# Output projection token tile by token tile, its norms beside it, and the MLP begun on half of the tokens

## The chip, the cores and the metric

The kernel runs on one core of a Trainium2 chip. The metric is the device time of one launch in microseconds (us). Before the change it is 1835.69 us, the median of three runs (1834.38 to 1842.27).

## What is computed

One layer of a transformer with an attention branch and a state-space branch, for 128 context tokens and 512 latent tokens of width 1024, all in float32. What matters here is the second half of the layer:

```
merged = sigmoid(g_a) * (attn @ w_attn_o) + sigmoid(g_b) * (y @ w_ssd_o)
mix    = merged @ w_out
x      = LN(alpha * x + gate1 * mix, ln1_g, ln1_b)       # LN: mean and variance over the 1024 columns
h      = LN(x) * (1 + scale2) + shift2
ff     = square(relu(h @ w_mlp1 + b_mlp1)) @ w_mlp2 + b_mlp2     # width 4096 between
x      = LN(alpha * x + gate2 * ff, ln2_g, ln2_b)
```

## The kernel before

The five engines run programs of their own, written out by hand in order; they meet only at semaphores. A matrix operand is split into an upper part (rounded to fp32r) and a lower part (the rest), so that a product is three matmuls: upper by upper, upper by lower, lower by upper. Weights come in blocks of 256 columns (1024 KB). SyncE loads a block into one of two slots of `raw`, ScalarE writes the upper part (`split_hi`, L1284, into `whi`), VectorE the lower one (`split_lo`, L1749, into `wlo`), and TensorE multiplies. Slot and parts of block b are b % 2. Tokens lie in five tiles of 128 (t = 0 is the context); activations that are the moving or stationary operand of a product lie turned, features on partitions, in `hh` (upper) and `hl` (lower), 8 slices k of 644 columns (640 tokens and 4 of padding). PSUM has two tensors of four banks, `acc` and `tp`.

The stretch that the change rewrites goes like this.

*Merge.* In four rounds TensorE multiplies y by two column groups (`sub`) of `w_ssd_o`. For each of the eight results VectorE multiplies by the gate (L2231) and adds the attention branch (L2234), ScalarE writes the upper part to `hh[:, k]` (`merged`, L1684), and VectorE the lower one (L2237, signal `merge_ok`). In the last round the splits of `w_out` blocks 0 and 1 stand between: on both ScalarE and VectorE, the split of block 1 comes ahead of the last merge.

*Output projection.* `pe.wait_ge(s["merge_ok"], KT)`, then `n_stream(2, hh, hl)`: the four blocks b of `w_out` in the outer loop, the five token tiles t in the inner one, 24 matmuls of 256 columns a unit, in two PSUM banks by turns. VectorE takes each unit out with the gate (L2258, into `x1[:, t, cols]`). From b = 2 on it also adds alpha * x and gathers statistics, 256 columns at a time.

*Norms.* When the last unit is out, VectorE goes over all tiles: means and deviations (`gathered`, `deviations`; the root is ScalarE's, L1291), the weighed norm (`weighed`, L1787 and L1788) and new statistics (`statistics`, L1767, L1769) tile by tile, deviations again, and the second norm (`normed`, L1791) into `xq`.

*Turn and modulation.* For each k TensorE turns five 128 by 128 pieces (`turn_x`, L847) into PSUM, ScalarE applies scale and shift (L1327, once for the 128 context tokens and once for the 512 latent ones) and writes the upper part (L1331), VectorE the lower one (`split_h`, L1825, signal `h2_ok`).

*MLP.* TensorE waits for all eight `h2_ok`. In four rounds it makes eight units of 48 matmuls of 322 columns (`t_unit`; each of the two halves of the tokens has its own bank), VectorE and ScalarE take them out with bias, relu and square (L2294, L2296, L1719, L2299, signal `ff_ok`), and then TensorE makes 4 x 5 units of the second product.

Of the kernel before, what the change touches and what calls it, by code (L numbers as in the profile page):

```python
# [6 lines left out]
F32 = mybir.dt.float32  # L7
# [6 lines left out]
P = 128  # L14
# [91 lines left out]
def build(nc, a, outs):  # L106
# [16 lines left out]
    with ExitStack() as ctx:  # L123
# [36 lines left out]
        class Carve:  # L160
# [134 lines left out]
        hf2 = cst[:, P:P + 2 * TP].rearrange("p (a b) -> p a b", a=2)  # L295
        lnr = c7(2, D)
        lnr2 = raw[:, 0].rearrange("p (a k) n -> p a (k n)", a=2)
        xq = c7(NT, D)

        acc = ctx.enter_context(nc.psum_tensor("acc", [P, 4, 512], F32))  # L300
        tp = ctx.enter_context(nc.psum_tensor("tp", [P, 4, 512], F32))

# [5 lines left out]
            conv_out0 conv_out1 dt_in dt_split dt_hi dt_mm dt_copied dt_turned dt_abs dt_soft dt_sums dt_summed  # L308
            dt_exp dt_ok dt_ln acst_ok acs_out kcr_in kct_out rot_ok
# [8 lines left out]
            merge_hi merge_ok gate_turned gate_copied gate_out rows2_in x1_ok h2_hi h2_ok relu_ok square_ok  # L318
# [18 lines left out]
        U_H2 = U_OUT + 4 * NT  # L337
        U_MLP = U_H2 + KT

# [20 lines left out]
        GATED = {8 + 2 * q: q for q in range(4)}  # L360

# [11 lines left out]
        def _(sp):  # L373
# [64 lines left out]
            sp.wait_ge(s["dt_hi"], 1)  # L438
# [211 lines left out]
            sp.wait_ge(s["h2_ok"], KT)  # L650
# [148 lines left out]
        def _(pe):  # L799
# [120 lines left out]
            pe.wait_ge(s["dt_split"], 1)  # L920
# [7 lines left out]
            last.then_inc(s["dt_mm"], 1)  # L928
# [28 lines left out]
            pe.wait_ge(s["dt_copied"], 1)  # L957
            for t in range(NT):
                last = pe.transpose(tp[:, 2, t * 2 * NH:(t + 1) * 2 * NH], dtt[:, tok(t):tok(t) + P], ident[0:2 * NH, 0:2 * NH])
            last.then_inc(s["dt_turned"], 1)  # L960
            qkv_block(1)
            pe.wait_ge(s["dt_sums"], 1)
# [8 lines left out]
            last.then_inc(s["dt_summed"], 1)  # L971
            qkv_block(2)
            pe.wait_ge(s["dt_ok"], 1)
# [289 lines left out]
            with rounds(pe, 4, (lo, 8), (ready, KT + 4 * NT), (free, KT + 4 * NT), (ff, KT)):  # L1263
                for n in range(KT):
                    if n % 2 == 0:
                        pe.wait_ge(lo["sem"], due(lo))
                    t_unit(n // 2 % 2, n % 2, n % 2, hh, hl)
                for n in range(KT):
                    pe.wait_ge(ff["sem"], due(ff))
                for b in range(4):  # L1270
                    pe.wait_ge(lo["sem"], due(lo))
                    n_block(b % 2, fh, fl)

        @block.scalar
        def _(act):
# [131 lines left out]
            act.activation(wdh[:], wdt, ACT.Copy).then_inc(s["dt_hi"], 1)  # L1407
            act.activation(alg, alg, ACT.Exp).then_inc(steps["sem"], step(steps))
            act.wait_ge(s["dt_mm"], 1)
            act.activation(dtt.rearrange("p (a b) -> p a b", a=2), tp[0:2 * NH, 0:2, 0:HALF], ACT.Copy).then_inc(s["dt_copied"], 1)  # L1410
# [23 lines left out]
            def decays_in(n):  # L1434
# [6 lines left out]
            act.wait_ge(s["dt_abs"], 1)  # L1441
            act.activation(dtu[:, 1], dtu[:, 0], ACT.Exp, scale=-1.0).then_inc(steps["sem"], step(steps))
            act.wait_ge(steps["sem"], value(steps))
            act.activation(dtu[:, 1], dtu[:, 1], ACT.Ln, bias=1.0).then_inc(s["dt_soft"], 1)
            block_out(1, q5[:, 1])
            act.wait_ge(s["dt_sums"], 1)
            act.activation(dtu[:, 1], dtu[:, 0], ACT.Ln).then_inc(s["dt_ln"], 1)
            act.wait_ge(s["dt_summed"], 1)
            act.activation(dec[:].rearrange("p t j h -> p j t h"),
                           tp[:, 1:4, 0:NT * 2 * NH].rearrange("p j (t h) -> p j t h", t=NT), ACT.Exp).then_inc(s["dt_exp"], 1)  # L1450
# [7 lines left out]
            act.wait_ge(s["dt_ok"], 1)  # L1458
# [241 lines left out]
            merge_round(3, split_hi)  # L1700

            with rounds(act, 2, (ready, 2 * NT), (hi, 2), (raws[0], 1), (raws[1], 1)):
                for b in range(2):
                    step(ready, NT)
                    act.wait_ge(ready["sem"], value(ready))
                    split_hi(b)
            roots(mv[:, :, 2])
            roots(mv[:, :, 2])
            jump(free, U_H2)
            act.wait_ge(s["pad_ok"], 2)  # L1710
            modulated(hf2, "h2_hi", "h2_ok", 4, 3)
# [24 lines left out]
        def _(dve):  # L1736
# [136 lines left out]
            dve.wait_ge(s["dt_hi"], 1)  # L1873
            dve.tensor_tensor(wdl[:], wdt, wdh[:].bitcast(F32), ALU.subtract).then_inc(s["dt_split"], 1)
# [39 lines left out]
            dve.wait_ge(s["dt_turned"], 1)  # L1914
            do(dve.tensor_tensor(dtu[:, 2], tp[:, 2, 0:NT * 2 * NH].rearrange("p (t h) -> p t h", t=NT), mid(dtb), ALU.add))
            do(dve.tensor_scalar(dtu[:, 0], dtu[:, 2], -1.0, None, ALU.mult))
            dve.tensor_tensor(dtu[:, 0], dtu[:, 0], dtu[:, 2], ALU.max).then_inc(s["dt_abs"], 1)
            do(dve.tensor_scalar(dtu[:, 2], dtu[:, 2], 0.0, None, ALU.max))
            squared(0)
            dve.wait_ge(s["dt_soft"], 1)  # L1920
# [3 lines left out]
            dve.tensor_scalar(dta[:], dta[:], -1.0, None, ALU.mult).then_inc(s["dt_sums"], 1)  # L1924
# [6 lines left out]
            dve.wait_ge(s["dt_exp"], 1)  # L1931
            dve.wait_ge(s["dt_ln"], 1)
# [3 lines left out]
            dve.tensor_tensor(sdt, dts[:], sdt, ALU.mult).then_inc(s["dt_ok"], 1)  # L1936
            dve.wait_ge(s["dt_ok"], 1)
# [286 lines left out]
            def merge_round(i, split):  # L2224
                split(0)
                for b in range(2):
                    dve.wait_ge(ready["sem"], due(ready))
                    if b == 1:
                        split(1)
# [12 lines left out]
            merge_round(3, split_lo)  # L2242

            dve.wait_ge(s["g1_in"], 32)

            def with_x(t, b):

                cols = slice(b * BW, (b + 1) * BW)
                do(dve.scalar_tensor_tensor(x1[:, t, cols], xo[:, t, cols], ALPHA, x1[:, t, cols], ALU.mult, ALU.add))
                dve.bn_stats(st6[:, t, b], x1[:, t, cols])  # L2250

            for b in range(4):
                cols = slice(b * BW, (b + 1) * BW)
                if b == 2:
                    dve.wait_ge(s["rows2_in"], 16 * 5)
                for t in range(NT):
                    dve.wait_ge(ready["sem"], due(ready))
                    dve.tensor_tensor(x1[:, t, cols], acc[:, 2 * ((NT * b + t) % 2), 0:BW],  # L2258
                                      g1r[:, min(t, 1), cols], ALU.mult).then_inc(free["sem"], step(free))
                    if b >= 2:  # L2260
                        dve.wait_ge(free["sem"], value(free))
                        with_x(t, b - 2)
                        with_x(t, b)
                split_lo(b % 2)
            for buf in (hf2[:, :, CTX:CTX + 2], hf2[:, :, NCONV:TP]):
                last = dve.memset(buf, 0.0)
            last.then_inc(s["pad_ok"], 1)
            for t in range(NT):
                gathered(t)
            deviations()  # L2270
            for t in range(NT):
                do(weighed(t, x1[:, t], lnr))
                statistics(t, x1[:, t])
            deviations()
            for t in range(NT):
                normed(t, xq[:, t], x1[:, t]).then_inc(s["x1_ok"], 1)
# [84 lines left out]
```

## Time and profile before

| | us |
|---|---|
| median of three runs | 1835.69 |
| the profiled execution, device time | 1839.19 |
| its span in the profile | 1837.5 |
| TensorE matmul busy in the span | 1632.3 (89%) |
| VectorE busy | 1031.7 (56%) |
| ScalarE busy | 663.7 (36%) |
| share of TensorE in the chain that ended last | 74% |

In the rows, PE is TensorE's matmul, PEld its weight load, DVE is VectorE, ACT ScalarE, SP SyncE. Times count from the start of the span. A releaser ("<-") is the instruction whose signal ended a wait.

### The profile page before, as it was taken

To read this page: it belongs to the slowest core of one execution; us is meant where nothing else is said; L and a number is where in the kernel's file an instruction comes from. 1 tells how busy PE (TensorE), PEld (TensorE's weight loads), DVE (VectorE), ACT (ScalarE), POOL (GpSimd) and SP (SyncE) were. 2 spreads that over 40 slices of the span, in tenths; PEclk is the share of its full clock that TensorE was granted. 3 is DMA by queue.
4 is the path that set the end of the run, shared out by engine and by line. 5 is a ranking of instruction groups with operands and counts; after the bars stand their busy time and mean duration, and the time that the engine had idled before them with its cause. 6 is when DMAs were issued, how large, how long until landed. Compare 5 with 4: busy or idle time off the path is not lost.

```text
span 1837.5 us, 27440 instructions
## 1 busy us (share of the span) xinstructions
PE 1632.3 (89%) x11141; PEld 1538.5 (84%) x11141; DVE 1031.7 (56%) x1419; ACT 663.7 (36%) x1115; POOL 99.3 (5%) x155
## 2 busy tenths in 40 slices
PE   4799999989998998989799899989299999999995
PEld 2699988889998988888655699989199999999995
DVE  5466666556845578887555353335843343342467
ACT  4544443334365246667355432311321121111210
POOL 1000012110011100000000001000000000000000
PEclk9799999899999999999899999999599999999998
DMA  9344345532486676676600255342011222223221
GB/s 309 99 134 136 124 142 187 174 116 75 138 264 206 221 241 213 200 240 189 236 23 23 71 184 179 112 174 70 23 44 56 84 68 68 68 68 91 69 68 57
DMA packets 159721, 241.14 MB, mean 131 GB/s; under 512 B 8048, under 2 KB 126560, under 8 KB 156576
## 3 DMA queue, kind: packets, MB, share of 16 engines
q1 hardware_dynamic: 136464, 171.45, 28.8%
q0 software_dynamic: 12304, 47.72, 7.0%
q10 hardware_dynamic: 10880, 20.97, 4.2%
q8 instruction: 49, 0.80, 0.2%
q14 instruction: 24, 0.20, 0.0%
HBM read 195.06 MB, written 45.06 MB: 131 GB/s over the span
## 4 chain that ended last, share of the span: by engine, by line
PE 74%; DVE 14%; ACT 7%; issue 2%; DMA 1%; SPq 0%; ACTq 0%; DVEq 0%
PE acc L806 66%; PE tp L806 6%; DVE arena L1849 2%; ACT arena L1510 1%; DVE wlo L1749 1%; PE tp L1188 1%; DVE arena L2002 1%; ACT whi L1284 1%; DMA arena<-in_w_mod 1%; DVE arena L1788 1%; DVE arena L1787 1%; PE tp L889 1%; DVE wlo L1800 1%; DVE arena L2004 1%; DMA y_nat<-arena 1%
## 5 line engine op out<-in xcount | busy, mean ns | idle before, releaser
L806 PE MATMUL acc<-hh,whi 128*128 128x322 f32 x1408 | 363.4, 325 | 16.6 <-DVE wlo L1749 7.2
L806 PE MATMUL acc<-hl,whi 128*128 128x322 f32 x1408 | 357.4, 321 | 0.0
L806 PE MATMUL acc<-hh,wlo 128*128 128x322 f32 x1408 | 354.9, 319 | 0.0
L806 PEld LDWEIGHTS acc<-hh,whi 128*128 128x128 f32 x1408 | 254.1, 198 | 18.7 <-issue 12.2
L806 PEld LDWEIGHTS acc<-hl,whi 128*128 128x128 f32 x1408 | 255.2, 198 | 0.0
L806 PEld LDWEIGHTS acc<-hh,wlo 128*128 128x128 f32 x1408 | 254.1, 197 | 0.0
L1284 ACT ACTIVATE whi<-raw 128x2048 fp32r<-128x2048 f32 x78 | 148.7, 1908 | 266.2 <-PE acc L806 266.2
L1749 DVE TENSOR_TENSOR wlo<-raw,whi 128x2048 fp32r<-128x2048 f32 x78 | 178.5, 2290 | 101.5 <-ACT whi L1284 101.2
L806 PE MATMUL acc<-whi,hh 128*128 128x256 f32 x720 | 206.9, 287 | 8.0 <-DVE hl L2237 8.0
L806 PE MATMUL acc<-whi,hl 128*128 128x256 f32 x720 | 203.6, 283 | 0.0
L806 PE MATMUL acc<-wlo,hh 128*128 128x256 f32 x720 | 203.6, 283 | 0.0
L806 PE MATMUL acc<-whi,fh 128*128 128x256 f32 x640 | 183.2, 286 | 15.2 <-DVE fl L2299 15.2
L806 PE MATMUL acc<-wlo,fh 128*128 128x256 f32 x640 | 183.3, 286 | 0.0
L806 PE MATMUL acc<-whi,fl 128*128 128x256 f32 x640 | 182.8, 286 | 0.0
L806 PEld LDWEIGHTS acc<-whi,hh 128*128 128x128 f32 x720 | 137.4, 191 | 8.8 <-issue 8.4
L806 PEld LDWEIGHTS acc<-whi,fh 128*128 128x128 f32 x640 | 124.5, 195 | 16.3 <-issue 16.3
L806 PEld LDWEIGHTS acc<-wlo,hh 128*128 128x128 f32 x720 | 137.0, 190 | 0.3
L806 PEld LDWEIGHTS acc<-whi,hl 128*128 128x128 f32 x720 | 137.0, 190 | 0.0
L806 PE MATMUL tp<-arena 128*128 128x64 f32 (+3 forms) x508 | 115.6, 373 | 15.0 <-DVE arena L2004 10.0
L806 PEld LDWEIGHTS acc<-wlo,fh 128*128 128x128 f32 x640 | 124.3, 194 | 0.0
L806 PEld LDWEIGHTS acc<-whi,fl 128*128 128x128 f32 x640 | 124.2, 194 | 0.0
L1849 DVE SCALAR_TENSOR_TENSOR arena<-arena,colp 128x642 f32<-128x642 f32 x128 | 113.7, 888 | 18.7 <-DVE arena L1847 1.2
(255 smaller groups left out, 2327.0 us busy)
## 6 DMA issues: line engine op xcount, KB each, us to landing
raw<-in_w_in SPq DMA_DIRECT2D x38, 1024.0 KB, 7.0
raw<-in_w_mlp SPq DMA_DIRECT2D x32, 1024.0 KB, 5.4
arena<-in_w_mod SPq DMA_DIRECT2D x24, 1024.0 KB, 6.3
arena<-decay_sums_t ACTq DMA_DIRECT2D x40, 512.0 KB, 5.5
arena<-xs_nat SPq DMA_DIRECT2D x8, 1024.0 KB, 8.0
raw<-in_w_ssd_o SPq DMA_DIRECT2D x8, 1024.0 KB, 6.0
y_nat<-arena POOLq DMA_DIRECT2D x6, 1024.0 KB, 7.2
arena<-y_nat SPq DMA_DIRECT2D x6, 1024.0 KB, 6.4
```

The source lines that it names most:

```text
L806: return pe.matmul(out, l, r, start=first, stop=last)
L889: last = pe.transpose(dst, cvs[:, n % 2, tok(t):tok(t) + P], ident)
L1188: last = pe.transpose(tp[:, j // 4, (j % 4) * P:(j % 4 + 1) * P], pr[:, u, j * P:(j + 1) * P], ident)
L1284: act.activation(whi[:, slot], raw[:, slot], ACT.Copy).then_inc(hi["sem"], step(hi))
L1510: last = act.activation(ee[:, b, d, r], abc[:, b, d, r], ACT.Relu, bias=dta[:, c, h:h + 1], scale=-1.0)
L1749: dve.tensor_tensor(wlo[:, slot], raw[:, slot], whi[:, slot].bitcast(F32), ALU.subtract).then_inc(lo["sem"], step(lo))
L1787: do(dve.scalar_tensor_tensor(x, x, mv[:, t, 0:1], rows[:, 0], ALU.subtract, ALU.mult))
L1788: return dve.scalar_tensor_tensor(x, x, mv[:, t, 2:3], rows[:, 1], ALU.mult, ALU.add)
L1800: dve.tensor_tensor(dst, src, upper.bitcast(F32), ALU.subtract).then_inc(mlo["sem"], step(mlo))
L1849: ins = dve.scalar_tensor_tensor(o, x[:, t:t + NCONV], w(t), o, ALU.mult, ALU.add)
L2002: last = dve.tensor_tensor(ee[:, b, d], ee[:, b, d], cbm[:, d, g].unsqueeze(1).broadcast_to([P, R, P]), ALU.mult)
L2004: dve.tensor_tensor(ee[:, b, 0], ee[:, b, 0], ee[:, b, 1], ALU.add).then_inc(m_ok["sem"], step(m_ok))
```

## The change

- **Last merges first.** In the last merge round ScalarE and VectorE do both merges before they split block 1 of `w_out`. TensorE no longer waits for all eight merges: units 0 and 1 of the output projection run over k = 0 to 6, each k behind its own `merge_ok`, and take k = 7 at their end.
- **Output projection by tiles.** The order of the twenty units becomes `OUT`: tiles 0, 1 and 2 mixed as far as the blocks arrive, then tile 3 and tile 4 with their four blocks each. All four blocks must now be kept: blocks 2 and 3 get parts of their own, `w2h` and `w2l`, where the operand of the merge product lay. The units go round four banks of `acc`.
- **Norms per tile.** VectorE takes units out (`gated_out`) and does, one tile behind the other, `summed` (add alpha * x over 1024 columns, statistics), `normed_once` (weighed norm, statistics) and `normed_twice` (the two numbers of the second norm). The second norm itself moves to ScalarE, which writes `xq`. The roots are per tile too, ten instead of two.
- **Turn and modulation per tile.** TensorE turns tile 0 behind unit 10, tile 1 behind unit 14, tile 2 behind unit 17, into `tp`; ScalarE modulates in eight instructions of 128 columns and writes the upper part in one of 1024 (`modulate`), VectorE the lower part in one (`lower`).
- **MLP from half the tokens.** Columns 0 to 321 hold the tokens of tiles 0, 1 and part of 2. TensorE waits for three tiles (`h2_ok` 3), makes the first halves of MLP units 0 to 3, turns tile 3 behind the first of them and tile 4 behind the last, and then makes the second halves. Units 2 and 3 use the banks of `tp` (`pair_of`), as every second pair of MLP units does now. For tile 4 VectorE does half of the modulation (`lower_last`).
- **Loads.** x, the weights of the norm and the bias row are asked for behind block 3 of `w_out`, in another order; their landing signals are split in two.
- Twelve semaphores of the dt stage become three, with the same order of waits.

```diff
@@ SyncE @@
+            sp.wait_ge(s["acc_ready"], U_OUT)
+            sp.dma_start(xo[:, 0], a["x_prompt"][0]).then_inc(s["xo_in"], 16)
+            sp.dma_start(lnr[:, 0], a["ln1_g"][0].partition_broadcast(P)).then_inc(s["xo_in"], 16)
+            sp.dma_start(lnr[:, 1], a["ln1_b"][0].partition_broadcast(P)).then_inc(s["xo_in"], 16)
+            sp.dma_start(xo[:, 1:NT], a["x_sample"][0].rearrange("(t p) d -> p t d", p=P)).then_inc(s["rows2_in"], 16)
             sp.wait_ge(s["merge_ok"], KT)
-            sp.wait_ge(s["acc_ready"], U_OUT)
-            sp.dma_start(xo[:, 0], a["x_prompt"][0]).then_inc(s["rows2_in"], 16)
-            sp.dma_start(xo[:, 1:NT], a["x_sample"][0].rearrange("(t p) d -> p t d", p=P)).then_inc(s["rows2_in"], 16)
-            sp.dma_start(lnr[:, 0], a["ln1_g"][0].partition_broadcast(P)).then_inc(s["rows2_in"], 16)
-            sp.dma_start(lnr[:, 1], a["ln1_b"][0].partition_broadcast(P)).then_inc(s["rows2_in"], 16)
             sp.dma_start(row, a["b_mlp2"][0].partition_broadcast(P)).then_inc(s["rows2_in"], 16)
@@ TensorE @@
+        OUT = [(0, 0), (1, 0), (2, 0), (0, 1), (1, 1), (0, 2), (0, 3), (1, 2), (1, 3), (2, 1), (2, 2), (2, 3)]
+        OUT += [(t, b) for t in range(3, NT) for b in range(4)]
+        TURN = {10: 0, 14: 1, 17: 2}
-            pe.wait_ge(s["merge_ok"], KT)
-            n_stream(2, hh, hl)
-            turn_x(xq, "x1_ok", NT)
-            pe.wait_ge(s["h2_ok"], KT)
+            for i in range(2):
+                out_begun(i, seen)
+                out_products(i, range(KT - 1))
+            for i in range(2):
+                out_products(i, [KT - 1]).then_inc(ready["sem"], step(ready))
+            for i in range(2, 4 * NT):
+                out_begun(i, seen)
+                out_products(i, range(KT)).then_inc(ready["sem"], step(ready))
+                if i in TURN:
+                    turn_tile2(TURN[i])
+            pe.wait_ge(s["h2_ok"], 3)
+            for n in range(4):
+                if n % 2 == 0:
+                    pe.wait_ge(lo["sem"], due(lo))
+                ...
+                half_unit(n, 0)
+                if n == 0:
+                    turn_tile2(NT - 2)
+            pe.wait_ge(s["acc_free"], U_OUT + 4 * NT)
+            turn_tile2(NT - 1)
+            pe.wait_ge(s["h2_ok"], NT)
+            for n in range(4):
+                half_unit(n, 1).then_inc(ready["sem"], step(ready))
+            for n in range(4, KT):
+                mlp_unit(n)
+            second_products()
+            with rounds(pe, 3, (lo, 8), (ready, KT + 4 * NT), (free, KT + 4 * NT), (ff, KT)):
+                for n in range(KT):
+                    mlp_unit(n)
+                second_products()
@@ ScalarE @@
-            merge_round(3, split_hi)
+            act.wait_ge(half["sem"], due(half))
+            split_hi(0)
+            gate_in(0)
+            gate_in(1)
+            merged(KT - 2)
+            merged(KT - 1)
+            step(ready, 2)
+            act.wait_ge(ready["sem"], value(ready))
+            split_hi(1)
+            for b in range(2):
+                act.wait_ge(raws[b]["sem"], due(raws[b]))
+                act.activation(w2h[:, b], raw[:, b], ACT.Copy).then_inc(hi["sem"], step(hi))
+            for t in range(NT):
+                roots(mv[:, t, 2:3])
+                if t:
+                    modulate(t - 1)
+                if t == NT - 2:
+                    act.wait_ge(ready["sem"], U_OUT + 17)
+                    split_hi(0)
+                roots(mv[:, t, 2:3])
+                if t == NT - 2:
+                    act.wait_ge(ready["sem"], U_OUT + 18)
+                    split_hi(1)
+                act.wait_ge(s["n2_ok"], t + 1)
+                act.activation(xq[:, t], x1[:, t], ACT.Identity, bias=mv[:, t, 3:4], scale=mv[:, t, 2:3]).then_inc(s["x1_ok"], 1)
+            modulate(NT - 1)
@@ VectorE @@
+            split_lo(1)
+            split_out_lo(0)
+            gated_out(3)
+            split_out_lo(1)
+            gated_out(4)
+            summed(0)
+            gated_out(1)
+            normed_once(0)
+            gated_out(1)
+            normed_twice(0)
+            summed(1)
+            gated_out(1)
+            normed_once(1)
+            gated_out(2)
+            for t in range(2, NT - 1):
+                lower(t - 2)
+                normed_twice(t - 1)
+                summed(t)
+                gated_out(2)
+                normed_once(t)
+                gated_out(2 if t == 2 else 1)
+            lower(2)
+            split_lo(0)
+            gated_out(1)
+            normed_twice(NT - 2)
+            summed(NT - 1)
+            split_lo(1)
+            normed_once(NT - 1)
+            normed_twice(NT - 1)
+            lower(NT - 2)
+            lower_last()
```

## Rows read from the trace of the kernel before

**Rows 1.** TensorE's waits, 1200 to 1400 us: waiter, releaser, total us, times, longest.
```profile
PE acc L847 <- DVE arena L1791: 32.3, 1, 32.3
PE acc L806 <- DVE hl L2237: 8.0, 1, 8.0
PE acc L806 <- DVE hl L1825: 4.2, 1, 4.2
PE acc L806 <- DVE fl L2299: 3.8, 1, 3.8
PE acc L847 <- ACT cst L1327: 2.5, 6, 0.5
```

**Rows 2.** Stretches: length, busy us (instructions) of PE, PEld, DVE, ACT, POOL; PEclk; DMA.
```profile
1220.60:1228.50 7.90, 0.02 (x1) 0.03 (x1) 4.68 (x4) 2.60 (x2) 0.00 (x0) 0.77 0.29 90
1228.50:1233.20 4.70, 4.70 (x28) 4.70 (x29) 0.08 (x1) 0.00 (x0) 0.00 (x0) 0.67 1.02 362
1233.20:1286.80 53.60, 53.56 (x455) 53.35 (x453) 28.74 (x59) 5.76 (x4) 0.00 (x0) 1.00 0.32 112
1286.80:1319.00 32.20, 0.00 (x0) 0.00 (x0) 30.52 (x50) 3.61 (x4) 0.00 (x0) 0.54 0.11 33
1319.00:1336.10 17.10, 10.36 (x40) 7.56 (x40) 10.05 (x14) 14.17 (x24) 0.00 (x0) 0.50 0.01 1
1336.10:1345.80 9.70, 9.66 (x50) 9.67 (x51) 0.00 (x0) 0.00 (x0) 0.00 (x0) 0.75 0.00 0
1345.80:1395.70 49.90, 49.90 (x336) 49.71 (x334) 24.72 (x24) 10.62 (x10) 0.00 (x0) 1.00 0.20 64
...
1399.60:1405.80 6.20, 6.19 (x29) 6.20 (x30) 2.71 (x2) 0.65 (x1) 0.00 (x0) 0.51 0.31 103
```

**Rows 3.** Chain that ended last, around the last merge: start, length, engine, line.
```profile
1220.56 1.92 ACT whi L1284
1222.60 2.29 DVE wlo L1749
...
1227.29 0.84 DVE hl L2237
...
1228.48 58.29 PE acc L806 x480
```

**Rows 4.** TensorE's turns in the chain, inside the attention projection (y).
```profile
1052.91 1.75 PE tp L1234 x16
```

**Rows 5.** DMA issues, 1224 to 1231 us: size of one, median us to landing.
```profile
raw<-in_w_out SPq DMA_DIRECT2D x1, 1024.0 KB, 5.1
...
arena<-in_b_mlp SPq DMA_DIRECT2D x1, 512.0 KB, 11.9
```

**Rows 6.** VectorE and ScalarE by form, 1289 to 1345 us: busy us, mean ns.
```profile
L1767 DVE BATCH_NORM_STATS2 st<-arena 128x6 f32<-128x512 f32 x10 | 6.4, 685 | 0.2
L1788 DVE SCALAR_TENSOR_TENSOR arena<-arena,mv 128x1024 f32<-128x1024 f32 x5 | 6.4, 1285 | 0.2
L1787 DVE SCALAR_TENSOR_TENSOR arena<-arena,mv 128x1024 f32<-128x1024 f32 x5 | 6.4, 1285 | 0.2
L1327 ACT ACTIVATE cst<-acc,modc 128x512 f32<-128x512 f32 x8 | 6.2, 769 | 0.0
...
L1327 ACT ACTIVATE cst<-acc,modc 128x128 f32<-128x128 f32 x8 | 3.5, 444 | 5.6 <-PE acc L847 5.6
...
L1769 DVE BATCH_NORM_AGGREGATE mv<-st 128x2 f32<-128x12 f32 x5 | 1.0, 209 | 0.2
...
L1777 DVE TENSOR_SCALAR mv<-mv 128x5 f32<-128x5 f32 x2 | 0.3, 172 | 0.1
```

**Rows 7.** VectorE's instructions by form over the whole span: busy us, mean ns.
```profile
L1749 DVE TENSOR_TENSOR wlo<-raw,whi 128x2048 fp32r<-128x2048 f32 x78 | 178.5, 2290 | 101.5 <-ACT whi L1284 101.2
...
L2258 DVE TENSOR_TENSOR arena<-acc,arena 128x256 f32<-128x256 f32 x20 | 8.4, 422 | 25.8 <-PE acc L806 25.7
...
L1910 DVE TENSOR_TENSOR arena<-arena,cst 128x1024 f32<-128x1024 f32 x5 | 6.1, 1226 | 0.2
```

**Rows 8.** ScalarE in order of time, 1319 to 1324 us: start, length of the pair.
```profile
1322.32 1.11 ACT L1327 ACTIVATE cst<-acc,modc 128x128 f32<-128x128 f32 x2
```

More of the change, by code:

```diff
@@ L1256, in _ @@
                     t_pass(1, sub, sub, yh, yl, KT, False, True).then_inc(ready["sem"], step(ready))
-            pe.wait_ge(s["merge_ok"], KT)
-            n_stream(2, hh, hl)
-            turn_x(xq, "x1_ok", NT)
-            pe.wait_ge(s["h2_ok"], KT)
-            ff = count(s["ff_ok"])
[L1263 to L1267, printed above, removed]
+            blocks = [(whi[:, 0], wlo[:, 0]), (whi[:, 1], wlo[:, 1]), (w2h[:, 0], w2l[:, 0]), (w2h[:, 1], w2l[:, 1])]
@@ new lines, in turn_tile2, with out_products @@
+            def turn_tile2(t):
+                pe.wait_ge(s["x1_ok"], t + 1)
+                if t >= 2:
+                    pe.wait_ge(s["h2_hi"], t - 1)
+                for k in range(KT):
+                    last = pe.transpose(turned_at(t, k), xq[:, t, k * P:(k + 1) * P], ident)
+                last.then_inc(s["h2_turned"], 1)
+            def out_products(i, ks):
+                t, b = OUT[i]
+                for k in ks:
+                    if i == 0:
+                        pe.wait_ge(s["merge_ok"], k + 1)
+                    for m, w in ((hh, 0), (hh, 1), (hl, 0)):
+                        last = mul(acc[:, i % 4, 0:BW], m[:, k, tok(t):tok(t) + P], blocks[b][w][:, k],
+                                   k == 0 and w == 0 and m is hh, k == KT - 1 and m is hl)
+                return last
@@ new lines, in mlp_unit @@
+            def mlp_unit(n):
+                if n % 2 == 0:
+                    pe.wait_ge(lo["sem"], due(lo))
+                step(free)
+                pe.wait_ge(free["sem"], value(free, 2))
+                for k in range(KT):
+                    for w, m in ((whi, hh), (whi, hl), (wlo, hh)):
+                        for half in range(2):
+                            last = mul(pair_of(n)[:, half, 0:HALF], w[:, n // 2 % 2, k, n % 2 * P:(n % 2 + 1) * P],
+                                       m[:, k, half * HALF:(half + 1) * HALF], k == 0 and w is whi and m is hh, k == KT - 1 and w is wlo)
+                last.then_inc(ready["sem"], step(ready))
@@ L2265, in _, with split_out_lo @@
[L2265 to L2271, printed above, removed]
+            def split_out_lo(b):
+                dve.wait_ge(hi["sem"], due(hi))
+                dve.tensor_tensor(w2l[:, b], raw[:, b], w2h[:, b].bitcast(F32), ALU.subtract).then_inc(lo["sem"], step(lo))
+            units = count(s["acc_ready"])
@@ new lines, in gated_out, with variance @@
+            def gated_out(n):
+                for i in range(units["k"], units["k"] + n):
+                    t, b = OUT[i]
+                    cols = slice(b * BW, (b + 1) * BW)
+                    dve.wait_ge(ready["sem"], due(ready))
+                    dve.tensor_tensor(x1[:, t, cols], acc[:, i % 4, 0:BW], g1r[:, min(t, 1), cols], ALU.mult).then_inc(free["sem"], step(free))
+                step(units, n)
+            def variance(t):
+                dve.tensor_scalar(mv[:, t, 2:3], mv[:, t, 1:2], EPS, None, ALU.add).then_inc(var["sem"], step(var))
@@ new lines, in summed, with normed_once @@
+            def summed(t):
+                dve.wait_ge(free["sem"], value(free))
+                if t == 0:
+                    dve.wait_ge(s["xo_in"], 48)
+                if t == 1:
+                    dve.wait_ge(s["rows2_in"], 32)
+                do(dve.scalar_tensor_tensor(x1[:, t], xo[:, t], ALPHA, x1[:, t], ALU.mult, ALU.add))
+                statistics(t, x1[:, t])
+                variance(t)
+            def normed_once(t):
+                dve.wait_ge(dev["sem"], due(dev))
+                do(dve.reciprocal(mv[:, t, 2:3], mv[:, t, 2:3]))
@@ L2272, in _, with normed_twice @@
                 do(weighed(t, x1[:, t], lnr))
                 statistics(t, x1[:, t])
[L2274 to L2276 removed]
+                variance(t)
+            def normed_twice(t):
+                dve.wait_ge(dev["sem"], due(dev))
+                do(dve.reciprocal(mv[:, t, 2:3], mv[:, t, 2:3]))
+                dve.scalar_tensor_tensor(mv[:, t, 3:4], mv[:, t, 0:1], -1.0, mv[:, t, 2:3], ALU.mult, ALU.mult).then_inc(s["n2_ok"], 1)
```

167 lines of the change are left out of this document (97 added, 70 removed).

## The prediction

> **What bounds the kernel now.** I read the waits of TensorE first, because it is 89% busy and every microsecond in which it stands still is likely to be on the path. In the stretch of the change they are few and long [rows 1]: 8.0 us for the lower part of the last merge (L2237), 32.3 us for the second norm (L1791), 2.5 us in six pieces inside the turn, and 4.2 us for the last lower part before the MLP (L1825). The 3.8 us for L2299 recur in each MLP round and are not touched.
>
> The stretches [rows 2] then say what lies around the waits. From 1233.2 to 1286.8 the output projection runs at the full clock (granted 1.00), 19 units in 53.6 us, 2.82 us each; VectorE is busy 28.7 of these 53.6 us and ScalarE 5.8, so both have room. From 1286.8 to 1319.0 TensorE does nothing and VectorE is busy 30.5 of 32.2 us. From 1319.0 to 1336.1 there are 40 turns at half clock, held to ScalarE's pace (14.2 of 17.1 us busy). The first MLP unit then takes 9.7 us (to 1345.8), and the seven that follow 49.9 us, 7.13 each. So from the end of the merge products, 1220.5, to the end of MLP unit 3 (1345.8 + 3 x 7.13 = 1367.2) there pass **146.7 us**. That is what I compare with; what comes behind unit 3 does not change.
>
> The chain [rows 3] shows why the last merge is late: it goes through ScalarE's split of block 1 (1.92 us from 1220.56) and VectorE's (2.29 us from 1222.60), and only then through the merge, which ends at 1228.1.
>
> **The change, part by part.** TensorE's own work after it, from 1220.5: 20 units x 2.82 = 56.4 us; five tiles turned, 8 turns each, with 16 turns in 1.75 us at full clock [rows 4], 5 x 0.88 = 4.4 us; eight half units = four units, 28.5 us. Together 89.3 us. To this come the waits, which I go through in order.
>
> *Last merge.* Units 0 and 1 over k = 0 to 6 last 2 x 7/8 x 2.82 = 4.9 us, to 1225.4. The merge now begins at 1220.5. In [rows 3] it takes from the end of the split (about 1224.8) to 1228.1, 3.3 us, so it is done at 1223.9. No wait; the cover is 1.5 us. The 8.0 us go, and with them the slow clock behind them.
>
> *Blocks 1 to 3.* ScalarE splits block 1 behind the last merge, 1223.0 to 1224.9, VectorE to 1227.2; unit 3 needs it at 1228.9. The upper part of block 2 follows on ScalarE, its lower part on VectorE is done at 1229.5, needed by unit 5 at 1234.5. Block 3 can be loaded only when VectorE has split block 1 (1227.2, where it was 1224.9). A block landed 5.1 us after its issue [rows 5]: 1232.4; 1.92 and 2.29 us for its parts [rows 3] give 1236.7. Unit 6 wants it at 1237.4. No wait, 0.7 us of cover. x and the norm rows are issued behind it; the last of that burst landed 11.9 us after its issue [rows 5]; with one block more ahead of it I say 15 us, so all is there by about 1244, and tile 1 wants it at about 1250. The blocks of the MLP queue behind and are wanted at 1279.
>
> *VectorE becomes the limit.* Unit 6 completes tile 0 at 1220.5 + 7 x 2.82 = 1240.2. From there on VectorE has no pause until TensorE may begin the MLP. Per tile: `summed` is one operation over 1024 columns and two half statistics, 1.29 + 2 x 0.66 + 0.21, with gaps and the 0.17 us of a tiny operation behind it 3.1 us; `normed_once` is a tiny one, two operations of 1.29 us and the same statistics, 4.6 us; `normed_twice` two tiny ones, 0.4 us [rows 6]. `lower` over 1024 columns is 1.25 us, taking out a unit 0.45 us, a split 2.29 us, each with its gap [rows 7]. Up to the lower part of MLP block 0 stand in its program 4 x 3.1 + 4 x 4.6 + 3 x 0.4 + 3 x 1.25 + 13 x 0.45 + 2.3 = 43.9 us: done at **1284.1**. TensorE by itself would be there at 1220.5 + 20 x 2.82 + 3 x 0.88 = 1279.5. **It waits 4.6 us.**
>
> ScalarE must not be late between. Eight modulations of 128 columns: one lasts 0.444 us [rows 6], and since a pair of 128 and 512 columns takes 1.11 us [rows 8] where the sum of both is 1.21, a series of eight is 0.34 to 0.44 us a piece, 2.8 to 3.6 us. The upper part over 1024 columns is about half of the 1.92 us for 2048 and some, 1.1; `xq`, by the step from 128 to 512 columns, 1.2. With the roots that is 5.5 to 6.3 us a tile; VectorE's share is 11. In the order of the waits the closest case is the second root of tile 2, which stands behind the modulation of tile 1: that ends at about 1269 and VectorE asks for the root at 1269. VectorE then still has units to take out and a lower part to write (2.1 us) before it needs the answer. So nothing.
>
> Here a rule of the Trainium skill speaks against the change: "VectorE: DVE Perf Modes", in its section on the TRN2 errata, says that ScalarE and VectorE pay a fixed cost for every instruction and wants tiles of 512 elements or more. The two forms of L1327 agree: from 512 to 128 columns the time falls only from 0.769 to 0.444 us. By the rule ScalarE's modulation rises from 9.7 us to about 36 x 0.44 = 16 us, but behind VectorE's longer program that changes no term.
>
> *First halves and last tile.* From 1284.1: half unit 0 3.57 us, tile 3 turned 0.9, half units 1 to 3 10.7 us. The clock will be low after a wait of 4.6 us: after the 3.8 us wait before 1399.6, 29 matmuls in 6.2 us ran at granted 0.51, which at full clock (0.118 us each) are 3.4 us, a loss of 2.8; after the 8.0 us wait the first unit lost 1.9 (4.7 us where 2.82 would do); the first MLP unit lost 9.7 - 7.13 = 2.6 us [rows 2]. I take 2.0 here. TensorE is ready to turn tile 4 at 1301.3. VectorE meanwhile: one unit out, 0.4, 3.1, a split 2.3, 4.6, 0.4 = 11.3 us, to 1295.4, then `xq` 1.2: 1296.6. So the last tile's norms are hidden, with 4.7 us of cover. What isn't: the turn, then on VectorE four operations of 128 columns (0.3 each), a copy and two subtractions of 512 (0.5 to 0.7 each): **3.1 us**. ScalarE's half (4 x 0.34 + 0.6) is shorter. I add 1.5 us for the clock again, less than before since the wait is shorter, and 0.5 us at MLP unit 4, which waits for VectorE to take out unit 2 behind a weight split.
>
> The sum: 89.3 + 4.6 + 2.0 + 3.1 + 1.5 + 0.5 = **101.0 us** instead of 146.7: 45.7 us less. The profiled execution would go from 1839.2 (1.7 us outside its span) to 1793.5. It lies 3.5 us above the median of the runs; the median would go to 1835.7 - 45.7 = **1790**.
>
> Bounds of what no row has. Clock losses: none to 2.8 each, -3.5 to +2.1 us. The many small steps of VectorE 7% cheaper or 10% dearer: -2.4 to +4.7. ScalarE's 128-column instructions: cheaper ones gain nothing; as dear as the 512-column form (6.1 us a tile), they push VectorE back by 4.9. The MLP keeps four waits of 3.8 us, whose clock losses (2.3 to 2.8) can fall otherwise by 2 us in all. Units 4 and later in other banks of `tp`: nothing, since the wait is still for the unit two back. The longer straight program of TensorE: nothing, since the attention and y stretch is written out too and runs its turns without gaps [rows 4]. The joined semaphores: nothing, the same order.
>
> **Rivals.** (a) *Block 3 lands late.* Its cover is 0.7 us, and the burst goes out in its back. For it: in [rows 5] the burst's last load took 11.9 us. Against: block 3 is asked for first. If it lands 3 to 7 us late, unit 6 waits 2 to 6 us, everything behind shifts, and the clock loses 2 more: 1794 to 1798.
>
> (b) *The two engines lock step.* ScalarE and VectorE hand roots, `n2_ok` and lower parts back and forth, each in program order; if each tile costs VectorE 2 to 4 us of waiting, four times, the limit moves from 1284 to 1292 or 1300, and with it everything behind: 1798 to 1806. Against it stand ScalarE's 5.5 to 6.3 us beside VectorE's 11.
>
> (c) *The output projection at half clock.* The new units wait on free banks and blocks, four banks round. If TensorE stood a little before every unit, its clock might stay at the 1.2 GHz level. The 29 slow matmuls in 6.2 us give 0.213 us against 0.118: over 480 matmuls 45.6 us, over 192 of the half units about 23 more, less the 4.6 us that TensorE then need not wait: 1790 + 64 = 1854, slower than before. It decides from about 480 slow matmuls on, the whole of the projection. Against: with the two-bank order the clock is 1.00 for 53.6 us without a break [rows 2], and my ledger has no wait in it. "TensorE: Matmul & The Clock Gate" in the Trainium skill, section on psum-queue depth-cycling, describes such a kernel, in which going round the PSUM banks leaves small pauses and the clock swings.
>
> (d) *The change does less than it says:* the first halves start only when the last tile is ready, as if there were no halves. Then the 14.3 us of first halves no longer lie beside the last tile's norms; less their present cover of 4.7 us that is 9.6 more: 1800. For it: the wait for tile 2's lower part and the block's split may drift towards the end of VectorE's program. Against: in that program they stand 11.3 us ahead of its last tile.
>
> **Chances.** The forecast, every wait as in the ledger within a few us: 0.70, its own range 1784 to 1797. (a) 0.10, (b) 0.10, (d) 0.03, (c) 0.02, and 0.05 for a larger gain, below 1784, if VectorE is quicker and the clock hardly falls. The range 1782 to 1802 leaves out (c), half of (b) and part of the last. A change of 0.5%, 9 us, is about what a measurement of this kernel can tell from none; only (c) and something like it would end there: faster 0.96, same 0.02, slower 0.02.
>
> **What would show it.** TensorE's waits between 1220 and 1320: no entry for the merge; one of about 4.6 us before the first half unit, released by L1749's split; one of about 3.1 before the second halves, released by the last lower part; none inside the twenty units. VectorE nearly without pause from 1240 to 1284. The granted clock 1.00 from 1216 to about 1279. MLP unit 3 ended at about 1321.5. I am wrong if the units of the projection show waits for blocks or for `x1_ok`, or if VectorE waits for ScalarE by more than 1 or 2 us in all from 1240 to 1284.

## The result

The changed kernel takes **1791.82 us** (median of 4 runs, 1787.32 to 1797.25) against 1835.75 us: a ratio of 0.9759, 95% interval 0.9741 to 0.9778, so 43.9 us less. The forecast was 1790. The profiled execution took 1791.86 us with a span of 1790.2.

TensorE's waits after it, from the last merge product to MLP unit 4 and the first `ff_ok`: waiter, releaser, total us, times, longest.

```profile
PE acc L821 <- DVE fl L2478: 4.0, 1, 4.0
PE acc L821 <- DVE hl L2428: 3.4, 1, 3.4
PE acc L821 <- issue: 2.6, 1, 2.6
PE acc L821 <- DVE cst L2473: 0.6, 1, 0.6
```

Of the four entries of [rows 1] that the change aims at, 47.0 us together, nothing is left under those names. There are two new waits, 2.6 us before the first half unit and 3.4 us before the second halves (L2428, the last lower part), and 0.6 us at MLP unit 4. The 4.0 us for L2478 is the old 3.8 us of L2299.

The stretches after it, with the columns of [rows 2]:

```profile
1216.10:1228.00 11.90, 11.90 (x103) 11.90 (x102) 7.97 (x8) 4.35 (x3) 0.00 (x0) 1.00 0.35 112
1228.00:1247.10 19.10, 19.10 (x164) 19.10 (x163) 14.12 (x24) 4.85 (x5) 0.00 (x0) 1.00 0.88 317
1247.10:1272.00 24.90, 24.90 (x215) 24.90 (x214) 23.14 (x45) 13.61 (x32) 0.00 (x0) 1.00 0.01 2
1272.00:1277.90 5.90, 3.34 (x29) 3.13 (x27) 5.58 (x9) 5.36 (x6) 0.00 (x0) 1.00 0.00 0
1277.90:1283.30 5.40, 5.37 (x26) 5.39 (x27) 5.26 (x9) 1.45 (x2) 0.00 (x0) 0.68 0.62 197
...
1294.80:1299.10 4.30, 0.92 (x9) 0.68 (x7) 3.23 (x8) 2.13 (x5) 0.00 (x0) 0.97 0.00 0
1299.10:1303.00 3.90, 3.90 (x17) 3.90 (x18) 3.33 (x5) 0.00 (x0) 0.00 (x0) 0.60 0.00 0
...
1315.70:1344.50 28.80, 28.80 (x192) 28.59 (x192) 16.15 (x16) 7.33 (x7) 0.00 (x0) 1.00 0.35 110
```

From 1216.1, the end of the merge products, TensorE runs to 1272 without a pause at granted 1.00; VectorE is busy 23.1 of the 24.9 us from 1247.1 to 1272.0, where it had been busy 28.7 of 53.6 [rows 2]. Behind the two waits the clock is at 0.68 and 0.60.

The forecast went wait by wait, and so does the comparison. From the last merge product to the start of MLP unit 4:

| term | forecast us | measured us |
|---|---|---|
| wait for the last merge | 0 | 0 |
| 20 units and 3 turned tiles | 59.0 | 59.2 (1216.1 to 1275.3) |
| 8 half units and 2 turned tiles at full clock | 30.3 | 30.3 (what the other rows leave) |
| wait before the first half unit | 4.6 | 2.6 |
| clock lost in it | 2.0 | 1.8 (5.4 where 3.57 would do) |
| wait before the second halves | 3.1 | 3.4 |
| clock lost behind it | 1.5 | 1.7 (16.0 from 1299.1 to 1315.1 where 14.3 would do) |
| wait at unit 4 | 0.5 | 0.6 |
| whole stretch | 101.0 | 99.6 (1216.1 to 1315.7) |

The stretch is 47.1 us shorter, the span 47.3. The part ahead was also 4.4 us shorter in this execution (the merge products ended at 1216.1, in [rows 2] at about 1220.5), and the part behind 4.2 us longer. Nothing shows the first to be an effect of the change: in the nine executions of the changed kernel and its variants profiled below this moment lies anywhere from 1212.5 to 1221.0, and in those of the kernel before and its two variants at 1220.5, 1216.0 and 1218.0. The second is an effect, and the forecast did not have it; the last experiments are about it.

VectorE in order of time, at the places that decide (start us, length, idle before and its releaser):

```profile
1216.13 0.83 DVE L2354 SCALAR_TENSOR_TENSOR arena<-arena,acc 128x644 f32<-128x644 f32 x1 [3.85 <-PE acc L821]
...
1218.63 0.83 DVE L2360 SCALAR_TENSOR_TENSOR hl<-arena,hh 128x644 fp32r<-128x644 f32 x1 [0.81 <-ACT hh L1778]
...
1230.38 2.29 DVE L2372 TENSOR_TENSOR out_lo<-raw,out_hi 128x2048 fp32r<-128x2048 f32 x1 [4.38 <-ACT out_hi L1819]
...
1235.89 0.42 DVE L2381 TENSOR_TENSOR arena<-acc,arena 128x256 f32<-128x256 f32 x1 [2.23 <-PE acc L821]
...
1252.37 0.15 DVE L2385 TENSOR_SCALAR mv<-mv 128x1 f32<-128x1 f32 x1
1252.44 0.74 DVE L2381 TENSOR_TENSOR arena<-acc,arena 128x256 f32<-128x256 f32 x2
1253.10 1.22 DVE L2413 TENSOR_TENSOR hl<-arena,hh 128x1024 fp32r<-128x1024 f32 x1
1254.23 0.16 DVE L2407 RECIPROCAL mv<-mv 128x1 f32<-128x1 f32 x1
1254.43 0.16 DVE L2408 SCALAR_TENSOR_TENSOR mv<-mv 128x1 f32<-128x1 f32 x1
1254.50 1.22 DVE L2394 SCALAR_TENSOR_TENSOR arena<-arena 128x1024 f32<-128x1024 f32 x1
...
1264.35 1.23 DVE L2413 TENSOR_TENSOR hl<-arena,hh 128x1024 fp32r<-128x1024 f32 x1 [0.76 <-ACT hh L1815]
...
1274.11 1.21 DVE L2413 TENSOR_TENSOR hl<-arena,hh 128x1024 fp32r<-128x1024 f32 x1
1275.54 2.29 DVE L1872 TENSOR_TENSOR wlo<-raw,whi 128x2048 fp32r<-128x2048 f32 x1 [0.21 <-ACT whi L1378]
...
1295.77 1.37 DVE L2421 TENSOR_SCALAR arena<-acc,modc 128x128 f32<-128x128 f32 x4 [5.96 <-PE acc L1280]
...
1298.36 0.69 DVE L2428 TENSOR_TENSOR hl<-arena,hh 128x512 fp32r<-128x512 f32 x1
```

The last merge starts at 1216.13 and its lower part ends at 1219.5, 3.3 us as forecast, when TensorE still has 1.5 us of k = 0 to 6 to do. Block 3 is split to 1232.7; its first unit was due at 1233.0, so about 0.3 us of cover were left where I had 0.7. At 1274.11 comes tile 2's lower part, then the split of MLP block 0, to 1277.83. TensorE's rows there:

```profile
1275.06 0.28 PE L821 MATMUL acc<-out_hi,hl 128*128 128x256 f32 x1
1277.93 0.39 PE L821 MATMUL acc<-hh,whi 128*128 128x322 f32 x1 [2.60 <-issue]
```

The view says "issue", as if nothing had held it, but the start at 1277.93 lies 0.1 us behind the end of the split, on whose signal the code waits. A releaser is inferred; the end times show it better here.

ScalarE (eight modulations and an upper part of tile 0, and the last `xq`):

```profile
1248.10 2.90 ACT L1811 ACTIVATE arena<-tp,modc 128x128 f32<-128x128 f32 x8 [0.17 <-PE tp L1280]
1251.03 1.06 ACT L1815 ACTIVATE hh<-arena 128x1024 fp32r<-128x1024 f32 x1
...
1288.70 1.25 ACT L1832 ACTIVATE arena<-arena,mv 128x1024 f32<-128x1024 f32 x1 [0.42 <-DVE mv L2408]
```

Eight modulations take 2.90 us, 0.36 each, inside the 0.34 to 0.44 of the forecast. The last `xq` is done at 1289.95, and TensorE turned that tile only at 1294.69:

```profile
1294.69 1.04 PE L1280 MATMUL acc<-cst,arena 128*128 128x128 f32 x8
```

That is 4.7 us of cover, as forecast.

### The profile page after: what moved, and what is told of

It is laid out like the page before. It is cut to its first block, busy times and chain, and to the rows that moved or that the text cites. A ratio compares the mean times of both kernels' runs of the same rounds, so it can differ in the third digit from the quotient of the medians.

```text
span 1790.2 us, 27388 instructions
## 1 busy us (share of the span) xinstructions
PE 1619.5 (90%) x11141; PEld 1528.4 (85%) x11141; DVE 1026.0 (57%) x1409; ACT 674.6 (38%) x1145; POOL 99.2 (6%) x155
## 4 chain that ended last, share of the span: by engine, by line
PE 75%; DVE 13%; ACT 7%; issue 3%; DMA 1%; SPq 0%; ACTq 0%; DVEq 0%
PE acc L821 60%; PE tp L821 12%; DVE arena L1972 2%; ACT arena L1604 2%; PE tp L1203 1%; DVE wlo L1872 1%; DVE arena L2125 1%; ACT whi L1378 1%; DMA arena<-in_w_mod 1%; PE tp L904 1%; DVE wlo L1923 1%; DVE arena L2127 1%; DMA y_nat<-arena 1%; ACT arena L1390 0%; ACT whi L1741 0%
## 5 line engine op out<-in xcount | busy, mean ns | idle before, releaser
L821 PE MATMUL acc<-hh,whi 128*128 128x322 f32 x1152 | 305.6, 327 | 22.7 <-DVE wlo L1872 7.2
L821 PE MATMUL acc<-hl,whi 128*128 128x322 f32 x1152 | 299.4, 321 | 0.0
L821 PE MATMUL acc<-hh,wlo 128*128 128x322 f32 x1152 | 297.5, 320 | 0.0
L821 PEld LDWEIGHTS acc<-hh,whi 128*128 128x128 f32 x1152 | 209.9, 199 | 25.3 <-issue 15.2
L821 PEld LDWEIGHTS acc<-hl,whi 128*128 128x128 f32 x1152 | 210.8, 198 | 0.0
L821 PEld LDWEIGHTS acc<-hh,wlo 128*128 128x128 f32 x1152 | 210.1, 198 | 0.0
L821 PE MATMUL acc<-whi,hh 128*128 128x256 f32 x640 | 183.8, 287 | 0.0
L821 PE MATMUL acc<-whi,hl 128*128 128x256 f32 x640 | 180.5, 282 | 0.0
L821 PE MATMUL acc<-wlo,hh 128*128 128x256 f32 x640 | 180.4, 282 | 0.0
L1390 ACT ACTIVATE arena<-acc 128x644 f32<-128x644 f32 (+2 forms) x94 | 47.8, 510 | 194.9 <-PE acc L821 194.8
```

The costliest lines, as they stand in the source:

```text
L821: return pe.matmul(out, l, r, start=first, stop=last)
L1390: act.activation(dst, src, func).then_inc(free["sem"], step(free))
```

## Experiments

All are compared with the kernel before on the same chip; medians of five or more runs. Ratios are to that kernel, and the changed kernel's own is 0.9759 (0.9741 to 0.9778). Because the front part drifts by some microseconds, I read the waits first and the medians second. "Stretch" below is from the last merge product until VectorE takes out MLP unit 4; it is 108.5 us in the changed kernel (109.6 in its second profile), 153.9 before. It ends later than the 99.6 us of the table above, which end where TensorE starts on unit 4.

No experiment takes back the tile order with the norms beside it, the largest part of the change. What it is worth rests on the traces: one wait of 32.3 us before, one of 2.6 us after.

### The order of the last merges alone

```diff
 (kernel before, ScalarE)
-            merge_round(3, split_hi)
+            act.wait_ge(half["sem"], due(half))
+            split_hi(0)
+            gate_in(0)
+            gate_in(1)
+            merged(KT - 2)
+            merged(KT - 1)
+            step(ready, 2)
+            act.wait_ge(ready["sem"], value(ready))
+            split_hi(1)
 (VectorE: the split of block 1 behind the last merge, too)
```

> The kernel before, with the order of the last merge round alone changed: both engines do the last merge before they split block 1. Theory (the last merge is late because it stands behind the two splits, 1.92 and 2.29 us in the chain): TensorE's wait at the start of the output projection falls from 8.0 to about 3.6 us, and the time by 4 to 5 us, to about 1831 us. Rival (the merge itself, or the gate's load, is what is late): the wait stays near 8 us and the time does not move.

1830.44 us, ratio 0.9966 (0.9950 to 0.9982).

```profile
PE acc L806 <- DVE hl L2245: 3.7, 1, 3.7
```

The wait went from 8.0 to 3.7 us, as the theory has it. The medians give 3 to 9 us by the interval, the wait 4.3, and the stretch is about 4 us shorter (150.1).

### The old order inside the changed kernel, and no early products

```diff
 (e5_old_merge_order, ScalarE; VectorE likewise)
             merged(KT - 2)
-            merged(KT - 1)
             step(ready, 2)
             act.wait_ge(ready["sem"], value(ready))
             split_hi(1)
+            merged(KT - 1)
 (e6_all_merges, TensorE)
-                        pe.wait_ge(s["merge_ok"], k + 1)
+                        pe.wait_ge(s["merge_ok"], KT)
```

> The changed kernel with the old order of the last merge round (block 1 split before the last merge), but TensorE still beginning units 0 and 1 with k = 0 to 6. Theory: these products cover 4.9 us, the merge is done about 7.6 us after the last merge product, so a wait of about 2.7 us appears in unit 0, with up to 2 us of clock behind it: 1794 to 1797 us. Rival (VectorE's chain alone sets when the MLP begins, so anything in front of it is hidden): 1792, no change.

> The changed kernel, but TensorE waits for all eight merges before unit 0 (the new order of the merges stays). Theory: the 3.4 us of the merge become a wait, and the clock may fall behind it for another 1 to 2 us: 1795 to 1797 us. Rival (the order alone does it, beginning with k = 0 to 6 is worth nothing, because VectorE's chain takes up the slack): 1792.

Old order: 1796.59 us, ratio 0.9784 (0.9759 to 0.9808). No early products: 1802.29 us, ratio 0.9807 (0.9780 to 0.9834). TensorE's wait for the last merge in the first and in the second:

```profile
PE acc L821 <- DVE hl L2360: 2.7, 1, 2.7
```

```profile
PE acc L821 <- DVE hl L2360: 3.6, 1, 3.6
```

2.7 and 3.6 us, where 2.7 and 3.4 were expected, and the other waits (2.6, 3.4, 0.6) keep their lengths behind it. So VectorE's chain does not swallow what is lost in front: its work hangs on unit 6, and unit 6 moves. With the old order the stretch is 111.6 us, 2 to 3 longer; the median lies in the expected range, but its interval overlaps that of the changed kernel. The stretch without early products is 113.6 us, 4 to 5 longer. Its median missed the expected 1795 to 1797 by 5 us; in its profiled execution, which is the median one, 5 us of the difference lie ahead of the stretch (merge products ended at 1221.0, in the changed kernel at 1216.1).

### No first halves

```diff
 (the loop over four first halves, with both turns, goes; in its place:)
+            turn_tile2(NT - 2)
+            pe.wait_ge(s["acc_free"], U_OUT + 4 * NT)
+            turn_tile2(NT - 1)
+            pe.wait_ge(s["h2_ok"], NT)
             for n in range(4):
+                if n % 2 == 0:
+                    pe.wait_ge(lo["sem"], due(lo))
+                half_unit(n, 0)
                 half_unit(n, 1).then_inc(ready["sem"], step(ready))
```

> The changed kernel without first halves: TensorE turns tiles 3 and 4, waits for the last lower part and then makes each MLP unit with both halves. Theory: the first halves are worth the 14.3 us that they fill less the 4 to 5 us in which the last tile was ready but not turned: 9 to 10 us dearer, 1801 to 1802 us. Rival (VectorE's chain would end at the same time and the halves only fill a wait that is as long anyway, with the clock kept up at most): within 3 us of 1792.

1801.65 us, ratio 0.9821 (0.9792 to 0.9849), in the expected range. The stretch is 116.6 us, only 7 to 8 longer, but this count hides a part: in the changed kernel VectorE takes out unit 4 about 1.8 us late, behind a weight split (until 1324.6). Up to TensorE's own start on unit 4 it is 109.3 us against 99.7 and 100.8 in the two profiles of the changed kernel, 8.5 to 9.6 longer, where I had said 9 to 10.

```profile
PE acc L1280 <- issue: 8.3, 1, 8.3
PE tp L1280 <- ACT arena L1825: 4.4, 1, 4.4
...
PE acc L821 <- DVE hl L2421: 3.4, 1, 3.4
```

16.1 us of waits around the turns of tiles 3 and 4, where the halves leave 6.0. The halves are real work put into that gap.

### The second norm on VectorE

```diff
 (ScalarE)
-                act.wait_ge(s["n2_ok"], t + 1)
-                act.activation(xq[:, t], x1[:, t], ACT.Identity, bias=mv[:, t, 3:4], scale=mv[:, t, 2:3]).then_inc(s["x1_ok"], 1)
 (VectorE, normed_twice; its last tiny operation no longer signals)
+                normed(t, xq[:, t], x1[:, t]).then_inc(s["x1_ok"], 1)
```

> The changed kernel with the second norm (xq) of every tile back on VectorE, about 0.75 us each instead of ScalarE's 1.25. Theory (VectorE's chain sets when the MLP may begin): four of the five lie ahead of the first half unit, so its wait grows by about 3 us, from 2.6 to 5.6, and the time by about 3 us: 1795. Rival (the hand-over between the engines is the limit, and one hop less helps): the wait does not grow, 1790 to 1792.

1794.63 us, ratio 0.9761 (0.9738 to 0.9784).

```profile
PE acc L821 <- issue: 3.6, 1, 3.6
```

The wait before the first half unit grew from 2.6 to 3.6 us, the stretch by 1 to 2. The direction is the theory's; the size is not. I had counted four norms ahead of that point, but `normed_twice(3)` stands behind the split, so there are three, 2.2 us. Of these 1.2 us fall into pauses that VectorE had in its chain, 1.0 us for ScalarE (0.76 and 0.21 in its rows above) and 0.2 for TensorE: in this trace none of them is left. That the median is the expected 1795 is luck: it can't be told from the changed kernel by its interval.

### x ahead of block 3

```diff
-            stream(2, w_out, 0)
+            for b in range(3):
+                block(w_out, 0, b)
 (the loads of x, ln1_g, ln1_b)
+            block(w_out, 0, 3)
```

> The changed kernel with the loads of x and of the norm rows (3.5 MB) issued ahead of block 3 of w_out instead of behind it. Theory (block 3 has less than 1 us of cover): it queues behind the burst, lands 2 to 3 us later, unit 6 waits 1.5 to 2.5 us, and all that follows shifts: 1793 to 1796. Rival (there is more cover than that, or VectorE's later wait absorbs it): no change, 1792.

1796.24 us, ratio 0.9777 (0.9752 to 0.9803); by the interval alone this can't be told from the changed kernel either.

```profile
PE acc L823 <- DVE out_lo L2374: 3.5, 1, 3.5
```

Block 3's lower part is now waited for by 3.5 us, more than the 1.5 to 2.5 expected, and the stretch is 113.6 us, 4 to 5 longer. Rival (a) of the prediction is real, and asking for block 3 ahead of the four other loads keeps it away.

### TensorE's stops at the back edges, and the last tile's turn

The 4.2 us behind the stretch: in the changed kernel TensorE stands at the two back edges of its loop over MLP rounds 1 to 3, 1.7 and 1.9 us, with no releaser.

```profile
1526.53 0.28 PE L821 MATMUL acc<-whi,fl 128*128 128x256 f32 x1
1528.52 0.56 PE L821 MATMUL acc<-hh,whi 128*128 128x322 f32 x2 [1.71 <-issue]
```

The kernels below write the loop out (e1_unrolled), turn the last tile earlier (e2_turn_early), or do both.

```diff
 (e1_unrolled)
-            with rounds(pe, 3, (lo, 8), (ready, KT + 4 * NT), (free, KT + 4 * NT), (ff, KT)):
+            for _ in range(3):
 (e2_turn_early)
                 if n == 0:
                     turn_tile2(NT - 2)
-            pe.wait_ge(s["acc_free"], U_OUT + 4 * NT)
-            turn_tile2(NT - 1)
+                if n == 2:
+                    pe.wait_ge(s["acc_free"], U_OUT + 4 * NT)
+                    turn_tile2(NT - 1)
 (e9_both: the two together)
```

> The changed kernel once more, on the chip of the next three, so that they can be compared with it. 1788 to 1796 us. In its MLP rounds TensorE stood for 1.7 and 1.9 us at two back edges of its loop with nothing to wait for; if that belongs to the program it is there again, if it was an accident of one execution it is not.

> The changed kernel with TensorE's loop over MLP rounds 1 to 3 written out, all else the same. Theory (the 1.7 and 1.9 us are the loop's back edges, instructions that are fetched late): both gaps go, 3 to 4 us less than the changed kernel beside it, about 1788 us. Rival (they come from the new PSUM banks or from the other engines' loops): the gaps stay, 1792. A written-out program could also be fetched late elsewhere: then the gaps move.

> The changed kernel with tile 4 turned behind the first half of MLP unit 2 instead of behind that of unit 3. Theory (the last tile's norms are done about 5 us before TensorE turns it, and only turn and modulation, 3.4 us, are uncovered): the first half of unit 3 covers them, the wait of 3.4 us and the slow clock behind it go: 3.4 to 5 us less, 1787 to 1788 us. Rival (x1_ok of the last tile comes just in time, so that the earlier turn waits itself): no change.

> Both edits of the last two kernels together. If both theories hold and the gains add: 6 to 9 us less than the changed kernel, 1783 to 1786 us.

Here the stretch and the time behind it are those of the one profiled execution of each.

| kernel | median us | ratio (interval) | stretch us | from unit 4 taken out to the end, us |
|---|---|---|---|---|
| changed, again | 1791.60 | 0.9763 (0.9747 to 0.9780) | 109.6 | 463.7 |
| written out | 1791.10 | 0.9741 (0.9724 to 0.9758) | 108.4 | 460.8 |
| turned early | 1791.96 | 0.9755 (0.9741 to 0.9769) | 103.5 | 465.5 |
| both | 1785.48 | 0.9721 (0.9702 to 0.9740) | 103.5 | 460.0 |

The changed kernel again has both gaps. The first is 1.66 us; the second carries a name, that of VectorE taking out a unit, but it stands at the same place, and written out it is gone with the first:

```profile
1650.19 0.56 PE L821 MATMUL acc<-hh,whi 128*128 128x322 f32 x2 [1.45 <-DVE arena L2485]
```

In all eight profiles of changed kernels that keep this loop both gaps are there, 1.45 to 2.02 us each.

Turned early, waits in the stretch and behind it up to the first `ff_ok`:

```profile
PE acc L821 <- DVE fl L2479: 4.0, 1, 4.0
PE acc L821 <- issue: 2.6, 1, 2.6
PE acc L821 <- DVE cst L2474: 0.6, 1, 0.6
```

The wait of 3.4 us is gone, and 5 to 6 us of the stretch with it, since the clock no longer falls there: granted 1.00 from 1283.5 to 1310. Written out, neither gap is there, and the rest is 3 to 5 us shorter. By the medians, each edit alone is lost in the spread, and both missed the times expected of them (about 1788, and 1787 to 1788). Together they give 1785.48 us, as expected and about 6 us below the changed kernel beside it, and the two intervals do not meet. That is the best kernel of this study.

Where do the gaps come from? The kernel before had a loop of four rounds and no gap in it. The change writes out round 0 and leaves a loop of three. That alone, in the kernel before:

```diff
-            with rounds(pe, 4, (lo, 8), (ready, KT + 4 * NT), (free, KT + 4 * NT), (ff, KT)):
+            def one_round():
                 (the body of the loop, unchanged)
+            one_round()
+            with rounds(pe, 3, (lo, 8), (ready, KT + 4 * NT), (free, KT + 4 * NT), (ff, KT)):
+                one_round()
```

> The kernel before, with TensorE's first MLP round written out ahead of a loop of three (instead of a loop of four), all else the same: the one thing about the MLP that the change alters in TensorE's program besides the banks. Theory (peeling the loop, not the banks or the halves, brings TensorE's stops at the two back edges): gaps of 1.5 to 2 us appear at the two remaining back edges, and the time from MLP unit 4 to the end grows by 2 to 5 us: 1839 to 1841 us beside 1836. Rival (another part of the change is needed for them): TensorE runs across the back edges without a gap, as in the kernel before, no change.

1841.18 us, ratio 1.0023 (1.0004 to 1.0041). TensorE's waits in the MLP, and the pieces of the chain on either side of the two back edges:

```profile
PE acc L806 <- DVE fl L2303: 15.3, 4, 4.0
PE acc L806 <- issue: 3.7, 2, 1.9
```

```profile
1517.50 59.00 PE acc L806 x480
1576.96 1.39 issue
1578.35 57.52 PE acc L806 x384
1639.68 59.31 PE acc L806 x480
1699.45 1.40 issue
1700.85 57.53 PE acc L806 x384
```

The gaps are there, 1.9 us each (the chain names 1.4 us of each as "issue"), so it is the peeling and neither the banks nor the halves. From unit 4 taken out to the end this kernel takes 468.2 us in its profile. With the loop of four it was 463.0 us in the kernel before and 460.8 in the one with the new merge order, whose MLP is the same. So the peeling costs 5 to 7 us there by the traces, somewhat more than the 2 to 5 expected, and 4.9 us by the medians (1836.31 beside it).

The profile also lists a queue, q8, that brings instructions. In the kernel before it moved nothing after 1516; peeled, it moves 9 packets in each later round, and in the changed kernel too. Since the peeling touched TensorE's program alone, the added packets are TensorE's. Written out, q8 moves 7 packets a round and there is no gap, so bringing instructions does not by itself stop TensorE; the stops come with the back edge. Why the loop of four does not fetch again and the one of three does, no run here says.

## Why the prediction was right

- *Last merge:* right, and shown by three kernels. The order is worth 4.3 us of wait, the early products the rest of the 8.0.
- *Blocks:* right, with about 0.3 us of cover for block 3 (forecast 0.7); letting four other loads go ahead of it turned this into a wait of 3.5 us.
- *VectorE as the limit:* right in kind, 2.0 us too long in size. The chain from unit 6 to the split took 41.9 us (1235.9 to 1277.8) and not 43.9. It holds 1.2 us of pauses that the sum had at nothing, so VectorE's own work was 40.7 us, 3.2 or 7% less than counted, which is the lower end of the bound that I gave. Operations that do not depend on each other follow faster than I counted: the tiny one at 1252.37 gives way after 0.07 us, two units are taken out in 0.66 us (0.9 in my sum), and the two tiny ones at 1254.23 take 0.27 (0.4). The bounds on this term were worked out wrong: 7% and 10% of 43.9 us are 3.1 and 4.4, not 2.4 and 4.7.
- *ScalarE:* right in the main. VectorE waited for it 1.0 us in all in that chain, where the sum had nothing and the prediction allowed 1 or 2. The bound of 4.9 us for dearer modulations has no working behind it, and the series came out at 0.36 us a piece. The rule of the Trainium skill on a fixed cost for every instruction ("VectorE: DVE Perf Modes", the section on the TRN2 errata) is seen in ScalarE's rows: 0.36 us for 128 columns in a series, and 0.769 for 512 before. That section speaks of operands in SBUF, and its table has a fixed part for those in PSUM too, from which these instructions read. It changed nothing in the time, since ScalarE had the room.
- *First halves and last tile:* right. The cover of the last tile's norms was 4.7 us (forecast 4.7), the uncovered end 3.4 (3.1). Without the halves TensorE starts on unit 4 later by 8.5 to 9.6 us.
- *Clock:* right. Losses of 1.8 and 1.7 us (2.0 and 1.5). Rival (c), the projection at half clock, did not occur: granted 1.00 for 56 us with four banks in turn. The psum-queue depth-cycling of "TensorE: Matmul & The Clock Gate" in the Trainium skill tells of small pauses between groups of matmuls; there were none here.
- *Wrong:* "The longer straight program of TensorE: nothing". The reason given for it, [rows 4], is one piece of 16 turns in a straight part; it says nothing of the loop that was left. The loop costs 3 to 5 us in the changed kernel, shown by writing it out, and the peeling alone brings the same stops into the kernel before.

The errors had different signs: 1.4 us too much for the stretch, 3 to 5 us too little behind it. The median was 1.8 us above the forecast; that it came so near is in part luck, since the two cancel in part.

## What to carry to other kernels

When several engines work in a fixed order, add up each engine's own instructions from the event that starts its backlog: here VectorE's sum, not TensorE's, gave the time at which the next stage could begin, to 2 us. A step that is late on its own account is cheap to move: if its input has been ready for some microseconds before it runs, move it forward by about that much, so that work already there covers what follows it (here one half unit further forward took away a wait of 3.4 us). And a loop whose first round is written out need not run as the whole loop did: look at its back edges in the trace.

## Seen on the way

- A back edge that cost nothing in a loop of four rounds was a stop of 1.9 us in a loop of three with the same body, and of 1.45 to 2.02 us in the changed kernels.
- Behind a wait of 2.6 us TensorE's granted clock was at 0.68 over the next 5.4 us, and behind 3.4 us at 0.60 over 3.9 us. This cost 1.8 and 1.7 us on top of the waits.
- The front part of one and the same program differs by up to 8.5 us from one execution to the next (last merge product at 1212.5 and at 1221.0 in two variants that differ only behind it).
